# Squarings and the inverse of a delta-rule recurrence on four 64x64 quadrants, with P + I as factor

## What is computed

```python
def rwkv7_time_mix(u, mu, w0, w_up, a0, a_up, g_up, k_k, k_a, r_k, ln_w, ln_b):
    ...
    y = rwkv7_scan(r_h, heads(decay), k_h, v_h, -kk, kk * a_h)
    mean = jnp.mean(y, axis=-1, keepdims=True)
    var = jnp.mean(jnp.square(y - mean), axis=-1, keepdims=True)
    ...
    return y.reshape(B, S, RWKV_W) * g
```

## Time and profile before

| | us |
|---|---|
| median of 3 runs | 2821.59 |
| lowest, highest | 2820.02, 2822.21 |
| span of the profiled execution | 2818.6 |
| first recurrence, iterations 0, 1 | 19.94, 19.91 |
| second recurrence, iterations 0, 1, 2 | 20.30, 19.81, 20.31 |
| second recurrence, iteration 3 with the tail | 30.48 |

### The profile page before, as it was taken

One profiled execution on the slowest core, in us unless ns is written; L12 is line 12 of the kernel. 1 busy time (PEld: TensorE's weight loads), 2 busy tenths in 40 slices (PEclk: granted clock), 3 DMA queues, 4 the chain that ended last, 5 costly groups with the idle time before them and its releaser, 6 DMA issues. The chain is left out here.

```text
span 2818.6 us, 48303 instructions
## 1 busy us (share of the span) xinstructions
PE 2765.8 (98%) x19892; PEld 2464.4 (87%) x19892; DVE 1955.9 (69%) x2715; ACT 1384.3 (49%) x2115; POOL 58.2 (2%) x45
## 2 busy tenths in 40 slices
PE   8999999999999999999999999999999999999998
PEld 7999888788999888999888778999888889888887
DVE  7887855676887876887855677788774469655541
ACT  4445544554544465544544555444555366444430
POOL 1000000001000001000000000100000000000000
PEclk9999999999999999999999999999999999999999
DMA  4334311103234241334222103233432211323331
GB/s 149 106 105 172 103 48 63 37 3 120 84 106 138 101 135 53 105 105 175 69 77 68 47 3 113 75 105 106 150 104 84 75 35 34 112 80 96 97 124 53
DMA packets 71065, 254.77 MB, mean 90 GB/s; under 512 B 7672, under 2 KB 8696, under 8 KB 70848
## 3 DMA queue, kind: packets, MB, share of 16 engines
q1 hardware_dynamic: 70848, 251.70, 26.9%
HBM read 249.57 MB, written 2.10 MB: 89 GB/s over the span
## 5 line engine op out<-in xcount | busy, mean ns | idle before, releaser
L261 PE MATMUL ps<-h_hi,w_space 128*128 128x512 f32 (+1 forms) x2624 | 697.2, 351 | 3.4 <-DVE h_lo L359 3.4
L271 PE MATMUL ps<-w_space 128*128 128x512 f32 x2448 | 567.3, 390 | 1.3 <-PEq L91 0.8
L271 PEld LDWEIGHTS ps<-w_space 128*128 128x128 f32 x2448 | 457.4, 188 | 96.1 <-issue 1.2
L261 PEld LDWEIGHTS ps<-h_hi,w_space 128*128 128x128 f32 x2624 | 462.4, 190 | 69.4 <-DVE h_lo L359 4.2
L249 DVE TENSOR_TENSOR w_space<-w_raw,w_space 128x1024 fp32r<-128x1024 f32 x256 | 311.9, 1231 | 258.7 <-ACT w_space L241 258.4
L261 PE MATMUL ps<-h_lo,w_space 128*128 128x512 f32 (+1 forms) x1312 | 456.9, 348 | 0.0
L942 PE MATMUL ps<-h_hi,w_space 128*128 128x256 f32 x2432 | 450.8, 283 | 0.0
L942 PEld LDWEIGHTS ps<-h_hi,w_space 128*128 128x128 f32 x2432 | 385.1, 192 | 0.2
L241 ACT CAST w_space<-w_raw 128x1024 fp32r<-128x1024 f32 x256 | 264.8, 1047 | 187.9 <-PE ps L261 102.9
L942 PE MATMUL ps<-h_lo,w_space 128*128 128x256 f32 x1216 | 344.1, 283 | 0.0
L261 PEld LDWEIGHTS ps<-h_lo,w_space 128*128 128x128 f32 x1312 | 249.3, 190 | 30.3 <-issue 0.5
(11 more groups left out here) (471 smaller groups left out, 3868.6 us busy)
## 6 DMA issues: line engine op xcount, KB each, us to landing
w_raw<-in_w_ffn_in SPq DMA_DIRECT2D x176, 512.0 KB, 3.7
w_raw<-in_w_in SPq DMA_DIRECT2D x64, 512.0 KB, 3.7
w_raw<-in_w_ffn_out SPq DMA_DIRECT2D x56, 512.0 KB, 3.7
w_raw<-in_w_up SPq DMA_DIRECT2D x44, 512.0 KB, 3.7
row_blocks<-in_w_ffn_out SPq DMA_DIRECT2D x8, 2048.0 KB, 11.8
w_raw<-in_w_out SPq DMA_DIRECT2D x24, 512.0 KB, 4.1
w_raw<-in_w_down SPq DMA_DIRECT2D x22, 512.0 KB, 3.7
w_raw<-in_w_ple_gate SPq DMA_DIRECT2D x16, 512.0 KB, 4.1
```

Of the source, the lines that this page charges most:

```text
L261: m = nc.tensor.matmul(c.ps[:, bank, t], part[:, cols], moving[:, k, t], start=(opens and k == 0 and i == 0), stop=(k == KD - 1 and i == 2 ...
L271: m = nc.tensor.matmul(c.ps[:, bank + half, :], x, part[:, half * S:(half + 1) * S], start=(first and i == 0), stop=(final and i == 2), sk ...
```

## The change

Half of the heads, the odd ones (q = 1), now change the partition half at each squaring: squares 2 to 5 and inverse steps 1 to 4 read row half r and write column half r XOR q. So a group of four matmuls goes to four quadrants. Square 1 and inverse 5 stay in their half, in the order row half 0 twice, row half 1 twice. PSUM bank q holds what belongs to heads of parity q: its first 256 columns are the squares, the next 128 the products with T. The addition of T is gone: VectorE makes the factor P + I from each power (the fifth straight from PSUM), and ScalarE copies the product to T. The fifth power is not copied any more. Banks 0 and 1 now serve both purposes, and waits keep a bank from being read while it is written: inverse i also waits for the copy of power i + 1, inverse 4 for factor 5, squares from 3 on for the T two steps back. `solve` writes to `SUM_BANK`, `local` to `Y_BANK` and `SCORE_BANK`, with waits of their own.

```diff
+                    if i >= 3:
+                        pe.wait_ge(t_ready, STEPS * t + i - 2)
+                    for o in range(2 if i < STEPS else 1):
+                        for j in range(2):
+                            at = (2 * o + j) * CHUNK
+                            for r, q in quadrants:
...
+                                m = nc.tensor.matmul(c.ps[half(r) if i == 1 else changed(r, q), q, at:at + CHUNK], (up, low)[o],
+                                                     (low, up)[o], start=True, stop=True)
...
-                    pe.wait_ge(power_ready, STEPS * t + i)
+                    if i < STEPS - 1:
+                        pe.wait_ge(power_ready, (STEPS - 1) * t + i + 1)
+                        pe.wait_ge(factor_ready, STEPS * t + i)
+                    else:
+                        pe.wait_ge(factor_ready, STEPS * (t + 1))
...
+                            m = nc.tensor.matmul(c.ps[changed(r, q) if i < STEPS else half(r), q, at:at + CHUNK],
+                                                 factor[half(r), i % 2, q, j, :], T[half(r), t % 2, q, j, :], start=True, stop=True)
...
+                def inverse(t, i):
+                    act.wait_ge(t_done, STEPS * t + i)
+                    nc.scalar.copy(T[:, t % 2].rearrange("p q j n -> p q (j n)"), c.ps[:, 0:2, T_COLS]).then_inc(t_ready, 1)
...
-                    nc.vector.tensor_tensor(T[:, t % 2], T[:, t % 2], by_head(quarter(T_BANK, 0)), ALU.add).then_inc(t_ready, 1)
+                def factors(t, i):
+                    if i < STEPS:
+                        dve.wait_ge(power_ready, (STEPS - 1) * t + i)
+                        src = power[:, i % 2, :, 0]
+                    else:
+                        dve.wait_ge(squared, STEPS * (t + 1))
+                        src = c.ps[:, 0:2, 0:P].rearrange("p q (j n) -> p q j n", j=2)
...
+                    nc.vector.tensor_tensor(factor[:, i % 2], src, masks[:, 3, :].unsqueeze(1).unsqueeze(1).to_broadcast(
+                        [P, 2, 2, CHUNK]), ALU.add).then_inc(factor_ready, 1)
```

More of the change, by code:

```diff
@@ L2327, in recurrence_stage @@
         heads = [(h, h // 2, half(h)) for h in range(R_HEADS)]
-        SQ_BANK, T_BANK, Y_BANK, MAX_BANK = 0, 1, 4, 6
+        Y_BANK, MAX_BANK = 4, 6
+        POWER_COLS, T_COLS = slice(0, 2 * P), slice(2 * P, 3 * P)
         out_bank = lambda t: Y_BANK if t < NT - 1 else SCORE_BANK
-        local_banks = (Y_BANK, T_BANK)
+        local_banks = (Y_BANK, SCORE_BANK)
+        quadrants = [(r, q) for r in range(2) for q in range(2)]
+        changed = lambda r, q: half(r ^ q)
         N_LOW, N_UP, AK = range(3)
@@ L2415, in inverse @@
                     else:
                         pe.wait_ge(t_ready, STEPS * t + i - 1)
-                    for h, j, rows in heads:
-                        for k in range(2):
-                            m = nc.tensor.matmul(c.ps[half(k), T_BANK, h * CHUNK:(h + 1) * CHUNK], parts(t, i)[0][half(k), h, :],
-                                                 T[half(k), t % 2, h, :], start=True, stop=True)
+                    for j in range(2):
+                        at = T_COLS.start + j * CHUNK
+                        for r, q in quadrants:
+                            m = nc.tensor.matmul(c.ps[changed(r, q) if i < STEPS else half(r), q, at:at + CHUNK],
+                                                 factor[half(r), i % 2, q, j, :], T[half(r), t % 2, q, j, :], start=True, stop=True)
@@ L2571, in _ @@
                     square(t, 2)
-                    inverse(t, 1)
                     if t >= 2:
@@ L2591, in _ @@
                         pairs_of_a(t + 1)
+                    inverse(t, 3)
                     scores(h, 2)
+                    square(t, 5)
                     if t:
                         outputs(t - 1)
-                    square(t, 5)
                     inverse(t, 4)
@@ L2714, in _ @@
                     powers(t, 2)
+                    inverse(t, 1)
                     if t == 0:
@@ L2725, in _ @@
                     powers(t, 3)
+                    inverse(t, 2)
                     weights(h, 1)
@@ L2930, in _ @@
                         local(t - 1)
+                    factors(t, 1)
+                    if t:
                         carry(2 * t - 2)
@@ L2937, in _ @@
                     exponent(h, 0)
-                    inverse(t, 1)
+                    factors(t, 2)
                     if t >= 2:
@@ L2942, in _ @@
                     weigh(h, 0)
-                    inverse(t, 2)
+                    factors(t, 3)
                     if t:
@@ L2948, in _ @@
                     weigh(h, 1)
-                    inverse(t, 3)
+                    factors(t, 4)
                     if t:
@@ L2961, in _ @@
                         sum_squares(h - 1)
-                    inverse(t, 4)
+                    factors(t, 5)
                     if more:
@@ L2968, in _ @@
                         mixout.y_lo(dve, nc, 1)
-                    inverse(t, 5)
                     weigh(h, 3)
```

79 lines of the change are left out of this document (39 added, 40 removed).

## The result

The changed kernel takes 2838.7 us (median of 4 runs, 2836.9 to 2842.5), the kernel before, run beside it, 2820.8. The ratio is 1.0064, 95% interval 1.0050 to 1.0079: slower by 18 us. The forecast was 2827.0 with a range of 2819 to 2836, so the time lies above the range. The direction given the larger chance (slower, 0.50) is right, and the size is wrong by 11.7 us.

The account below looks back on a forecast made before the run. TensorE, busy 98%, bounds the kernel, but VectorE's and ScalarE's queues turn its saving into waiting. Two layers x 2.2 plus 1.0 for the clock gave +5.4 us, span 2824.0, median 2827.0 us, range 2819 to 2836.

Parts of the forecast that it names:

- TensorE, what is saved: Squares 2 to 5 and inverses 1 to 4 at the corner products' four-quadrant pace: 2.2 us per iteration, 17 over eight.
- Rival 3: Four quadrants miss the corner pace because both row halves write one bank; TensorE saves nothing, 2835 us; chance 0.08.
- Iteration 0, the queues: In t=0, later table load and factor 5 delay inverses 2 and 4: net +2.2 us per layer, bounds 1.8 and 2.7.
- Iterations 1 and 2: In t=1 and 2 TensorE's saving becomes waiting: 0 us, bounds -0.4 and +0.6.
- If VectorE were 0.7 us quicker in that run: VectorE's gapless run from weigh(0) to the sum of squares, 7.34 us; 0.7 quicker and the gain appears at once.
- Iteration 3: In t=3 and the tail, the chains by which TensorE waits are not shortened: 0 us, bounds -0.8 and +0.5.
- The clock: TensorE idle in iterations 0 and 3 brings likelier one more half-clock stretch, net, than none: +1.0 us.
- half of 2.15: Price taken for a half-clock stretch: scores(0) to solve takes 15.55 us in the first recurrence, 13.40 in the second.
- 1: TensorE is the only bound and the other queues follow: gain 17 us, time 2804; chance 0.05.
- 2: Waits shorter than thought, no extra clock stretch: -1.4 us per layer, time 2818.8; chance 0.13.
- 4: A A D D slower than A D A D on two quadrants: 0.73 us an iteration, +5.8, time 2832.8; chance 0.08.

Follow-up runs that it names:

- e1: Changed kernel with every product of squares and inverses kept in its own partition half, two quadrants instead of four: 2842.0 us, ratio 1.0064.
- e9: Kernel before with TensorE's program in the changed kernel's order (inverses apart from squares, square 5 ahead of outputs), no quadrants, no P + I: ratio 1.0009.
- e8: e1 with the two halves alternating from one matmul to the next, A D A D instead of A A D D: gives 0.35 us back; total time not given.
- e5: Changed kernel with matmuls nobody reads, sized to stay inside TensorE's waits in t=0 and t=3: 2829.2 us, ratio 1.0031.
- e3: Changed kernel with ScalarE's floor and Exp table load moved ahead of its copy of inverse 1 in t=0: 2838.1 us.
- e6: Changed kernel with factor 5 moved in VectorE's queue from behind weigh(2) and the squares' sums to ahead of weigh(2): 2832.1 us, ratio 1.0037.
- e15: Changed kernel with matmuls nobody reads in t=3's waits alone (2 ahead of inverse 2, 3 of scores(1), 3 of outputs(2)): 2833.7 us.
- e4: Kernel before with one unread ScalarE copy ahead of the floor and table load in t=0, so that TensorE waits: 2826.1 us, ratio 1.0016.
- e12: Changed kernel with the row half changing from one matmul to the next: t=1 at 19.94 us instead of 20.04; total time not given.
- e7: Changed kernel with both e3's and e6's moves of order: 2840.8 us, ratio 1.0069.
- e10: e7 with matmuls nobody reads in waits: 5 and 2 in t=0, 2, 3 and 3 in t=3: 2819.5 us, ratio 0.9993.

## Why the prediction was wrong, step by step

**TensorE, what is saved: right at the pace, too large in sum.** A square of 16 takes 0.52 us (forecast 0.56). An inverse step takes 0.39 and a square of 8 takes 0.52 up to their successors (forecast 0.28 each) where a change of shape follows; inverse 4, which has 64x64 work behind it, takes 0.28 (1663.98 to 1664.26). In t=1 TensorE's busy time fell by 1.47 us, not 2.2: the quadrants give 2.7 (after against e1), and the new order and program take back 1.2. Of these, 0.28 is the new order (e9; the step had two pieces "about 0.1 us each"), 0.4 the order A A D D on two quadrants (busy 20.88 against 20.46, e1 against e8), and 0.5 is not separated. Rival 3 (no corner pace) is false. The Trainium skill, page TensorEngine Tiling (Array Packing), Restrictions and Gotchas, says that different row tiles cannot access the same PSUM bank simultaneously; if they took turns here, the groups of four starts within 20 ns, with both row halves in one bank, could not come about, so the trace disagrees for these shapes.

**Iteration 0, the queues: right.** Forecast: table load 1.6 us later, TensorE idle nearly 3 ahead of inverse 2, over 1.5 ahead of inverse 4, net +2.2 per layer. Measured: 1.74 later, 2.79, 1.26, and by e5, which has the waits and not the half clock, +2.58 and +2.18 us. (The step's own terms put inverse 4 at 1633.7, not 1633.6, which changes nothing.) The 1.26 is small only because TensorE came to it late at half clock; the 2.3 us of e5 are what the forecast's "over 1.5" speaks of. e3 and e6 show both causes to be the places in the queues that the forecast named.

**Iterations 1 and 2: small miss.** Forecast 0, bounds -0.4 and +0.6; measured +0.24, +0.22 in layer 1 and +0.22, +0.43 in layer 2, 1.1 us in all, each inside the bounds. "If VectorE were 0.7 us quicker in that run, the gain would appear at once" was right: e6 takes factor 5 out of the end of that run, and t=1 falls to 19.05.

**Iteration 3: right at full clock, by one reading.** Forecast 0, bounds -0.8 and +0.5; e15 in layer 2 has 30.52 us with the order as changed, before had 30.48. Its t=2 took 20.90 us, though, where 20.25 is usual: TensorE pauses late in it (0.37 us at 1688.24, with no releaser in the profile), so that t=3 starts later than usual against VectorE's work. Iterations 2 and 3 together are 51.42 us against 50.79 before.

**The clock: the term that failed.** The step said "likelier one more, net, than none", at "half of 2.15: +1.0". The cause and the places were right, t=0 and t=3 behind waits. The size was wrong in both its factors. The number: I counted one more for the whole kernel, and there were stretches in t=0 and t=3 of both layers, six against one. The price: the sum took 1.0 us for a place, and 10.2 us at half clock cost 2.7 us in t=0 (25.23 against 22.5) and 3.0 to 3.3 in t=3 (33.85 and 33.54 against 30.52; 2.7 to 2.9 if t=2 and t=3 are taken together, 54.10 and 54.28 against 51.42). Even the 2.15 called the upper price was below that, since it was of a stretch of 6.8 us (2.16 against layer 2, 1.87 against the 30.77 of e4). Sum: 2.71 + 2.75 in t=0, 3.33 + 3.02 - 2.16 in t=3, together +9.7 us instead of +1.0. The Trainium skill, page TensorE: Matmul & The Clock Gate, Part 1, says that the clock's ratio is set by how busy TensorE has been recently; e4 and e5 agree, the one by a wait added without the change, the other by the waits of the change filled. With waits of 4.8 (forecast 4.4), 1.1 in t=1 and 2 (forecast 0) and 0.1 for the work of t=3, this makes the 15.6 us by which the recurrences grew. The remaining 0.9 of the span lies outside them, where a stretch of 3.4 us at 2299.57 is in the profile after and not in that before; that it is the cause is not shown.

The mistake behind it was one of reasoning. A kernel whose profile shows a half-clock stretch in one layer's t=3 and none in the other's, with the same program, is, I would now argue, close to that edge in both. That it comes and goes is seen in e4, whose t=3 is untouched and has none in either layer. I took the one stretch as a price and not as a sign of how little more waiting it takes. The wait of nearly 3 us, forecast for both layers, was twice as long as any wait of TensorE in the recurrences before (1.46 us), so a stretch was to be expected in each layer and not in one of them. "Since most of the time there is then set by VectorE and ScalarE" was wrong in part. For the first stretch of t=0 there is something in it: 6.8 us at half clock cost some 1.4 there, since the wait ahead of inverse 4 became shorter. But behind inverse 4 TensorE runs to the end of t=0 without a wait, in 7.8 us in e5 and in 9.1 in the changed kernel, where the second half-clock stretch lies there: 3.4 us of it cost 1.35.

**The rivals.** 1 and 2 had the sign wrong. 4 is false in size: 0.1 us an iteration by e12, not 0.73. With four quadrants too, TensorE starts some records ahead of others that stand before them in its program (two of L2453 at 1688.47, the last three of L2409 from 1688.48), so it keeps its order less strictly than "The kernel before" says.

What stays open: why some stretches last 24 to 27 us (e3, e7) and others 3.4 to 10.2 in the same place. TensorE is busy 21.46 of 23.90 us in such a stretch, and e10 shows only that it does not come when the waits around it are filled. Open too is when a wait of middle length brings a stretch and when not (see the last section).

## What to carry to other kernels

When a change makes TensorE wait where it did not, add the clock to the wait: for each place and each execution of the stage a stretch at half clock, priced from a stretch at either level in the same trace, and not once for the kernel. When a forecast says that a gain on TensorE turns into waiting, it has said that the clock may fall; then mend the queues that make it wait (a table load, a copy, a small product behind a long run), and if waits are left, matmuls that nobody reads can be cheaper than the waits. To tell waits from clock, fill the waits: e5 and e10 answered in one run each what the totals of e3 and e7 hid.

## What the runs showed of the hardware

- TensorE's granted clock fell to 0.50 in or within 1.5 us of the end of each of the 14 waits of 1.94 to 2.80 us that the 18 profiles have in the recurrences. Of their 35 waits of 1.0 to 1.8 us, 18 had such a fall within 1.8 us and 17 had none. In t=3 of the changed kernel it fell behind waits of 0.34 and 0.57 us, in one of 0.86; in t=1 and 2 of the same kernel, with waits of 0.57 and 0.86 us, it never fell.
- The stretches lasted from 3.4 to 27.3 us, and 10.2 us of them cost 2.7 to 3.3 us of time.
- Filling 15 matmuls of 0.22 us into the waits of a recurrence made a kernel 21 us faster (e7 to e10).
- Four quadrants, with both row halves writing one bank, ran a square of 32 records in 0.52 us; two quadrants take 0.98.
- Taking the row halves in turn instead of two and two gives 0.35 us an iteration where two quadrants are used (e8 against e1) and 0.1 where four are (e12 against after).
